# Experts written out, weight stream reordered, outputs summed in PSUM: the mixture-of-experts stage of a two-block transformer kernel

## The chip, the cores and the metric

The kernel runs on one core of a Trainium2 chip. A core has TensorE (PE in the profile, with PEld for its weight loads), VectorE (DVE), ScalarE (ACT), GpSimd (POOL) and SyncE (SP, which issues DMAs), an on-chip memory SBUF of 128 partitions, and PSUM, eight banks of 128 x 512 fp32 into which TensorE writes. Each engine works through its own instructions in order; semaphores tie the engines together. The metric is the device time of one execution in microseconds (us), lower is better.

## The reference

A first block (modulated token mixer with gated delta rule and gated linear attention, then a mixture of experts) and a second block of two attention layers. Only the expert layer matters here: 256 tokens, 32 experts, each token goes to its 4 best; each expert is three 1024 x 1024 fp32 matrices (gate, linear, down), 12 MB.

```
logits = (h @ w_router + b_router)
top_logit, top_idx = lax.top_k(logits, TOP_K); top_p = jax.nn.softmax(top_logit)
# tokens packed by expert, then for each block of tokens xb of expert e:
gu = xb @ w_gu[e] + b_gu[e]
glu = jnp.minimum(gu[:, :D_EXPERT], SWIGLU_LIMIT)
lin = jnp.clip(gu[:, D_EXPERT:], -SWIGLU_LIMIT, SWIGLU_LIMIT)
act = glu * jax.nn.sigmoid(SWIGLU_ALPHA * glu) * (lin + 1.0)
return (act @ w_down[e] + b_down[e]) * p[:, None]
# summed over the experts of each token
```

## The kernel before

`route` computes the router, the gates and each token's rank within its expert. An expert takes up to 64 tokens (SLOTS); tokens beyond that go to a second pass (`further`), which does no expert work in this trace.

`one_pass` runs the 32 experts as a loop on every engine. The weights come as 12 units of 1 MB (512 rows x 512 columns) per expert, in a ring of 12 buffers. To keep fp32 accuracy with the faster fp32r products, each unit is split: ACT copies it, rounded, into one of six `moe_hi` buffers (line 1699); the rest, raw minus hi, is formed in place (line 1488), by DVE for nine units and by POOL for units 2, 6 and 10; then PE multiplies with both parts, 8 matmuls of 512 columns a unit (lines 1522 and 1523). The stationary operand holds the expert's tokens twice, 64 columns of high parts and 64 of low parts.

Around that, for each expert:
- DVE makes the one-hot matrix `pick` of token against slot (line 1588) and `pickg`, the same times the gate (line 1646).
- PE gathers the tokens with `pick` (line 1514, fp32, 32 matmul records for 16 matmuls), ACT and DVE split the result into `moe_xs` (1691, 1601).
- Units 0 to 7 give gate and linear columns, half by half; ACT copies each bank to `gu_tok` (1703), PE transposes (`turn`, 1534), DVE adds the halves and the bias (1608, 1612), clips (1615, 1616), ACT takes the sigmoid (1707), DVE forms the product and splits it into `acs` (1621 to 1627).
- Units 8 to 11 are the down matrix, with `acs` stationary; ACT copies the result to `y_tok` (1687), PE scatters it to the tokens with `pickgT` (1544) and DVE adds it to `yT` in SBUF (1596). Result and scatter of an expert are done inside the next iteration.

The order on each engine is that of the code in each engine's `body`. PE's products of a unit wait for its rest part; ACT's rounding of a unit waits until the unit six places earlier has been used by PE.

## Time and profile before

| | |
|---|---|
| median of 3 runs | 4019.8 us (4016.48 to 4021.62) |
| profiled execution | 4024.09 us, span 4022.3 us |
| granted TensorE clock, mean | 0.854 of full |
| PE busy | 3078.3 us, 77% |
| DVE busy | 2429.5 us, 60% |
| ACT busy | 1645.2 us, 41% |
| POOL busy | 752.9 us, 19% |

The expert stage lies between about 1320 and 2636 us of the span, a third of the kernel. Busy times are of the whole span, so what bounds this stage has to be read from views of the stage alone. A matmul's end in the trace is modelled and matmuls overlap: the distance from start to start is what each one costs.

### The profile page before, as it was taken

The page shows a single profiled execution, that of the slowest core. Times are in us where ns is not written, and L with a number is a line of the kernel's source. Part 1 is how long each engine was busy: PE and PEld are TensorE (multiplying, and loading weights), DVE is VectorE, ACT ScalarE, POOL GpSimd, SP SyncE. Part 2 cuts the span into 40 slices and gives each one's busy share as a digit, 9 for nine tenths or more (in the row PEclk, how much of TensorE's full clock was granted, in tenths as well). Part 3 has the DMA queues.
Part 4 walks back from the last instruction along what each step waited for, and adds up shares of the span by engine and source line. Part 5 has one row for each costly group of instructions (what it writes and reads, how often), then busy time and mean ns, then how long its engine had stood idle before and what let it go on. Part 6 is the DMA issues. An engine that isn't in the chain of part 4 may idle for free. (4 is left out here: it accounts for less than half of the span.)

```text
span 4022.3 us, 51270 instructions
## 1 busy us (share of the span) xinstructions
PE 3078.3 (77%) x17216; PEld 2524.4 (63%) x17217; DVE 2429.5 (60%) x3532; ACT 1645.2 (41%) x2098; POOL 752.9 (19%) x272
## 2 busy tenths in 40 slices
PE   7689999888676788888888888838336987625788
PEld 2368888566476667666767676728224987622688
DVE  1235545343354798989898989845544554454555
ACT  0024444211132576767777777713111442211343
POOL 0022232000000344444544454500000000000000
PEclk9789999877787899999999999969556998755899
DMA  7241100111141888888888888733001542200443
GB/s 261 76 76 32 32 22 1 34 35 59 46 150 49 329 319 315 303 319 302 323 301 321 303 320 299 250 105 111 1 1 51 159 167 84 79 0 0 141 142 104
DMA packets 323602, 605.74 MB, mean 151 GB/s; under 512 B 21858, under 2 KB 79769, under 8 KB 323353
## 3 DMA queue, kind: packets, MB, share of 16 engines
q1 hardware_dynamic: 318300, 598.43, 43.3%
q10 hardware_dynamic: 5181, 5.76, 0.5%
q8 instruction: 68, 1.11, 0.1%
q14 instruction: 53, 0.43, 0.0%
HBM read 599.75 MB, written 4.39 MB: 150 GB/s over the span
## 5 line engine op out<-in xcount | busy, mean ns | idle before, releaser
L1488 POOL TENSOR_TENSOR moe_raw_r<-moe_raw,moe_hi 128x2048 fp32r<-128x2048 f32 x96 | 609.5, 6349 | 1306.3 <-ACT moe_hi L1699 1306.3
L1699 ACT ACTIVATE moe_hi<-moe_raw 128x2048 fp32r<-128x2048 f32 x384 | 708.9, 1903 | 1.9 <-DMA moe_raw<-in_w_gu 1.5
L1488 DVE TENSOR_TENSOR moe_raw_r<-moe_raw,moe_hi 128x2048 fp32r<-128x2048 f32 x288 | 681.5, 2393 | 29.0 <-DVE acs L1627 19.2
L1522 PE MATMUL banks<-moe_hi,moe_xs 128*128 128x512 f32 x1024 | 410.1, 400 | 34.7 <-DVE moe_raw_r L1488 27.7
L1523 PE MATMUL banks<-moe_raw_r,moe_xs 128*128 128x512 f32 x1024 | 401.2, 392 | 0.0
L1522 PE MATMUL banks<-moe_hi,acs 128*128 128x512 f32 x512 | 248.8, 486 | 169.1 <-DVEq L1630 121.0
L319 PE MATMUL banks<-ff_xs,ff_hi 128*128 128x272 f32 x1024 | 300.9, 294 | 70.3 <-DVE ff_raw_r L335 61.0
L321 PE MATMUL banks<-ff_xs,ff_raw_r 128*128 128x272 f32 x1024 | 298.5, 291 | 0.0
L320 PE MATMUL banks<-ff_xs,ff_hi 128*128 128x272 f32 x1024 | 298.0, 291 | 0.0
L1522 PEld LDWEIGHTS banks<-moe_hi,acs 128*128 128x128 f32 x512 | 119.7, 234 | 222.3 <-issue 134.4
L1522 PEld LDWEIGHTS banks<-moe_hi,moe_xs 128*128 128x128 f32 x1024 | 193.3, 189 | 96.0 <-DVE moe_raw_r L1488 41.7
L319 PEld LDWEIGHTS banks<-ff_xs,ff_hi 128*128 128x128 f32 x1024 | 196.0, 191 | 74.2 <-issue 62.3
L1523 PE MATMUL banks<-moe_raw_r,acs 128*128 128x512 f32 x512 | 235.9, 461 | 0.0
L1523 PEld LDWEIGHTS banks<-moe_raw_r,moe_xs 128*128 128x128 f32 x1024 | 193.4, 189 | 38.3
L320 PEld LDWEIGHTS banks<-ff_xs,ff_hi 128*128 128x128 f32 x1024 | 196.5, 192 | 0.0
L321 PEld LDWEIGHTS banks<-ff_xs,ff_raw_r 128*128 128x128 f32 x1024 | 196.2, 192 | 0.0
L732 PE MATMUL banks<-hT,wq 128*128 128x256 f32 (+1 forms) x512 | 181.3, 497 | 4.6 <-PEq L161 2.1
L321 PE MATMUL banks<-sc_r,ring_att_r 128*128 128x272 f32 x608 | 180.2, 296 | 0.0
L319 PE MATMUL banks<-sc_r,PT_r 128*128 128x272 f32 x304 | 94.7, 311 | 91.7 <-DVE ring_att_r L335 88.5
L1707 ACT ACTIVATE sg<-gu 128x256 f32<-128x256 f32 x64 | 26.7, 418 | 323.5 <-DVE gu L1615 323.5
L1646 DVE TENSOR_SCALAR pickg<-con,rankr,gate 128x128 f32<-128x128 f32 x64 | 156.9, 2490 | 0.0
L335 DVE TENSOR_TENSOR ff_raw_r<-ff_raw,ff_hi 128x1024 fp32r<-128x1024 f32 x128 | 156.0, 1219 | 0.0
(471 smaller groups left out, 6553.2 us busy)
## 6 DMA issues: line engine op xcount, KB each, us to landing
moe_raw<-in_w_gu SPq DMA_DIRECT2D x256, 1024.0 KB, 7.9
moe_raw<-in_w_down SPq DMA_DIRECT2D x128, 1024.0 KB, 5.1
ff_raw<-in_w_ff SPq DMA_DIRECT2D x128, 512.0 KB, 3.8
ring_mod<-in_w_mod SPq DMA_DIRECT2D x12, 2048.0 KB, 8.7
wq<-in_w_in SPq DMA_DIRECT2D x32, 512.0 KB, 4.1
ring_att<-in_w_in SPq DMA_DIRECT2D x32, 512.0 KB, 3.7
ring_att<-in_w_in SPq DMA_DIRECT2D x32, 448.0 KB, 3.7
wh<-in_w_in SPq DMA_DIRECT2D x10, 1024.0 KB, 8.5
```

Source lines behind the costliest of these rows:

```text
L319: pe.matmul(ps[m][:, :n], w_hi, x_hi, start=(k == 0), stop=False)
L320: pe.matmul(ps[m][:, :n], w_hi, x_lo, start=False, stop=False)
L321: ins = pe.matmul(ps[m][:, :n], w_lo, x_hi, start=False, stop=(k == KT - 1))
L335: dve.tensor_tensor(lo[:, k, :cols], raw[:, k, :cols], hi[k % RING_HI][:, :cols].bitcast(F32), ALU.subtract).then_inc(los, 1)
L732: ins = pe.matmul(out, wq[:, h % 2, n, k, :], hT[:, k, lo:TOK], start=(k == 0), stop=(k == KT - 1))
L1488: eng.tensor_tensor(rest[u][:, :, :], raw[u][:, :, :], hi[:, u % HI_SLOTS, :, :].bitcast(F32), ALU.subtract).then_inc(sem, 1)
L1522: pe.matmul(bank, x[:, k, :], hi[:, u % HI_SLOTS, k, :], start=first, stop=False)
L1523: ins = pe.matmul(bank, x[:, k, :], rest[u][:, k, :], start=False, stop=last)
L1646: ins = dve.tensor_scalar(pickg[:, t, :], con[:, K_SLOT:K_SLOT + P], rank, gate[:, t, bass.ds(e, 1)], ALU.is_equal, ALU.mult)
L1699: act.activation(hi[:, u % HI_SLOTS, :, :], raw[u][:, :, :], ACT.Copy).then_inc(his, 1)
L1707: act.activation(sg[:, :, :], g[:, 0, :, :], ACT.Sigmoid, scale=ALPHA).then_inc(sig, 1)
```

## The change

The 32 experts are no longer a loop; their code is written out on each engine. A unit is now 256 rows x 1024 columns (still 1 MB). The stream order is a list: after the first expert's gate and linear columns it goes, for each expert e, gate columns of e+1 (g), down matrix of e (d), linear columns of e+1 (u). The first 12 units are issued in `route`. DVE forms all rest parts; POOL has no work in this stage. A pair of PSUM banks (0,1 or 2,3, in turn) takes all products of an expert; banks 4 to 7 collect the output of all experts, first b_down times gates, then each expert's scatter as accumulating matmuls, so that DVE's additions to `yT` go. The gather works on tokens that `route` has already split (32 fp32r matmuls of 64 columns). The transposes of gate and linear columns become matmuls with `fold` that also add high and low halves. `pickg` goes; instead PE transposes `pick` and multiplies the gates into a column per slot (`slots_of`), which ACT uses as the scale when it copies the result. The outputs end as tokens x columns, so a short stage after the loop transposes them back.

```diff
+def stream_order():
+    out = [("g", 0, q) for q in range(4)] + [("u", 0, q) for q in range(4)]
+    for e in range(NEXP):
+        if e + 1 < NEXP:
+            out += [("g", e + 1, q) for q in range(4)]
+        out += [("d", e, q) for q in range(4)]
+        if e + 1 < NEXP:
+            out += [("u", e + 1, q) for q in range(4)]
...
+        def first_units(sp):
+            for n in range(UNITS):
+                load_unit(sp, n)
...
+        def gather(pe, hot_one, bank):
+            for k in range(KT):
+                for x, c in ((h_hi, 0), (h_lo, SLOTS)):
+                    for t in range(2):
+                        ins = pe.matmul(ps[bank + k // 4][:, k % 4 * P + c:k % 4 * P + c + SLOTS], x[:, t, k * P:(k + 1) * P],
+                                        hot_one[:, t, 0:SLOTS], start=(t == 0), stop=(t == 1))
...
+        def slots_of(pe, hot_one, gates, bank):
+            for t in range(2):
+                pe.transpose(ps[bank][:, t * P:(t + 1) * P], hot_one[:, t, :].bitcast(F32), ident)
+            for t in range(2):
+                ins = pe.matmul(ps[bank][:, LAT:LAT + 1], hot_one[:, t, :].bitcast(F32), gates(t), start=(t == 0), stop=(t == 1))
...
+            @block.tensor
...
+                def scatter(e):
+                    pe.wait_ge(y_out, e + 1)
+                    for t in range(2):
+                        for c in range(2):
+                            ins = pe.matmul(ps[4 + 2 * t + c][:, :], pickT[:, t * P:(t + 1) * P], y[:, c * 512:(c + 1) * 512],
+                                            start=False, stop=(e == NEXP - 1))
...
+                for e in range(NEXP):
+                    nxt = e + 1 < NEXP
+                    if nxt:
+                        pe.wait_ge(x_out, e + 2)
+                        for q in range(2):
+                            unit("g", e + 1, q)
+                    turn(e, 1)
+                    if nxt:
+                        for q in range(2, 4):
+                            unit("g", e + 1, q)
+                    pe.wait_ge(t_free, 2 * e + 2)
+                    for q in range(4):
+                        if q % 2 == 0:
+                            pe.wait_ge(act_ready, 2 * e + q // 2 + 1)
+                        unit("d", e, q)
+                    if nxt:
+                        pe.wait_ge(gu_out, 2 * e + 3)
+                        for q in range(4):
+                            unit("u", e + 1, q)
+                            if q == 1:
+                                scatter(e)
+                            if q == 2:
+                                slots_in(e + 1)
+                        if e + 2 < NEXP:
+                            pe.wait_ge(s_out, e + 2)
+                            fetch(e + 2)
+                        pe.wait_ge(gu_out, 2 * e + 4)
+                        turn(e + 1, 0)
...
+            @block.scalar
...
+                def rounded(n):
+                    act.wait_ge(loaded[n % UNITS], n // UNITS * 16 + 16)
+                    if n >= HI_SLOTS:
+                        act.wait_ge(used, n - HI_SLOTS + 1)
+                    act.activation(hi[n % HI_SLOTS][:, :], raw[n % UNITS][:, :], ACT.Copy).then_inc(his, 1)
...
+                for e in range(NEXP):
...
+                    if nxt:
+                        rounded(g0)
+                        if e:
+                            results(e - 1)
+                        for q in range(1, 4):
+                            rounded(g0 + q)
+                    slots_out(e)
+                    rounded(d0)
+                    out("u", e)
+                    rounded(d0 + 1)
+                    if nxt:
+                        x_of(e + 1)
+                    rounded(d0 + 2)
+                    sigmoid(e, 0)
+                    rounded(d0 + 3)
+                    if nxt:
+                        rounded(u0)
+                        out("g", e + 1)
+                        rounded(u0 + 1)
+                    sigmoid(e, 1)
+                    if nxt:
+                        rounded(u0 + 2)
+                        rounded(u0 + 3)
...
+            @block.vector
...
+                for e in range(NEXP):
...
+                    if nxt:
+                        lo(g0, g0 + 1)
+                    act_first(e, 0)
+                    if nxt:
+                        lo(g0 + 2)
+                    act_second(e, 0)
+                    if nxt:
+                        lo(g0 + 3)
+                    act_first(e, 1)
+                    lo(d0)
+                    act_second(e, 1)
+                    lo(d0 + 1, d0 + 2, d0 + 3)
+                    if nxt:
+                        lo(u0)
+                        if e + 2 < NEXP:
+                            dve.wait_ge(slots, e + 1)
+                            hot_of(e + 2)
+                        lo(u0 + 1, u0 + 2, u0 + 3)
...
+        with stage(nc, "yt_sb yt_mm yt_v") as (block, in_sb, mm, on_dve):
```

PE, before, from the gather of the next expert (L1514) to the second transposes (L1534) and the down units, inside the loop body; the REGISTER_ALU and ISA rows compute what is waited for:

```order
L1511 REGISTER_ALU
L1514 MATMUL banks<-pick,htok 128x128 x16
L1561 REGISTER_ALU
L1563 MATMUL banks<-con,pickg 128x128 x2
L1527 REGISTER_ALU
L1529 ISA
L1534 MATMUL banks<-con,gu_tok 128x128 x8
L1566 REGISTER_ALU
L1484 REGISTER_ALU
L1522 MATMUL banks<-moe_hi,acs 128x512
```

PE, after, from the end of the second linear unit through the scatter (L1572), the third unit, the slots (L1518, L1520) to the start of the fourth; further on, the last rows of the gather (L1509) and the turn (L1564):

```order
L1550 MATMUL banks<-moe_raw_r,moe_xs 128x512 x2
L1572 MATMUL banks<-y_tok,pickT 128x512 x4
L1550 MATMUL banks<-moe_hi,moe_xs 128x512 x2
L1550 MATMUL banks<-moe_raw_r,moe_xs 128x512 x2
L1550 MATMUL banks<-moe_hi,moe_xs 128x512 x2
L1550 MATMUL banks<-moe_raw_r,moe_xs 128x512 x2
L1518 MATMUL banks<-con,pick 128x128 x2
L1520 MATMUL banks<-gate,pick 128x1 x2
...
L1509 MATMUL banks<-pick,htok_lo 128x64 x2
L1564 MATMUL banks<-con,gu_tok 128x64 x8
L1550 MATMUL banks<-moe_hi,moe_xs 128x512 x2
```

The scatter, which stood in the middle of an expert's eight gate and linear units, now stands with the slots, the gather and the first turn in the last three linear units and right behind them.

DVE, before, from the last rest part ahead of the additions to `yT` to the second half of the activation:

```order
L1488 TENSOR_TENSOR moe_raw_r<-moe_raw,moe_hi 128x2048
L1593 REGISTER_ALU
L1595 REGISTER_ALU
L1596 TENSOR_TENSOR yT<-yT,banks 128x512
...
L1608 TENSOR_TENSOR gu<-banks,vec 128x512
L1432 ISA
L1612 TENSOR_TENSOR gu<-gu,banks 128x512
L1432 REGISTER_ALU
L1615 TENSOR_SCALAR gu<-gu 128x256
L1616 TENSOR_SCALAR gu<-gu 128x256
L1487 REGISTER_ALU
L1488 TENSOR_TENSOR moe_raw_r<-moe_raw,moe_hi 128x2048
```

DVE, after, from the rest parts of d1, d2, d3 and u0 (the first `x4`), the one-hot rows of the expert after next, u1, then u2, u3 and the next g0 and g1 (the second `x4`) to the first half of the activation, with g2 inside it (rows L1693 are rest parts; `moe_yT_r` is the sixth rounded buffer, `y_tok_r` is the memory of `acs`):

```order
L1693 TENSOR_TENSOR moe_raw_r<-moe_raw,moe_hi 128x2048 x4
L1525 TENSOR_SCALAR pick<-con,rankr 128x128 x2
L1693 TENSOR_TENSOR moe_raw_r<-moe_raw,moe_yT_r 128x2048
L1693 TENSOR_TENSOR moe_raw_r<-moe_raw,moe_hi 128x2048 x4
L1703 TENSOR_TENSOR gu<-banks,vec 128x512
L1707 TENSOR_SCALAR gu<-gu 128x256
L1708 TENSOR_SCALAR gu<-gu 128x256
L1693 TENSOR_TENSOR moe_raw_r<-moe_raw,moe_hi 128x2048
L1713 SCALAR_TENSOR_TENSOR gu<-gu 128x256
L1715 TENSOR_TENSOR gu<-gu,sg 128x256
L1717 CAST y_tok_r<-gu 128x4x64
L1719 TENSOR_TENSOR y_tok_r<-gu,y_tok_r 128x4x64
```

Between the activation of one expert and that of the next DVE now has nothing but rest parts and one pair of one-hot rows; the additions to `yT`, the `pickg` rows and the second addition of halves are gone, and three rest parts an expert have come from POOL.

## Rows read from the trace of the kernel before

**Rows 1.** Stage table: us; busy PE, PEld, DVE, ACT, POOL; clock; DMA share; GB/s

```profile
1336.10:2589.30 1253.20, 1061.05 (x5017) 855.20 (x5017) 1119.49 (x1055) 900.37 (x715) 590.85 (x94) 0.94 0.88 316
```

**Rows 2.** Timeline (start, length, engine, line, operation), ACT, first and 32nd result copy

```profile
1336.10 1.00 ACT L1687 ACTIVATE y_tok<-banks 128x1024 f32<-128x1024 f32 x1
...
2589.28 1.03 ACT L1687 ACTIVATE y_tok<-banks 128x1024 f32<-128x1024 f32 x1 [0.65 <-PE banks L1523]
```

**Rows 3.** Timeline of DVE over one expert; in brackets idle before and its releaser

```profile
2007.88 0.69 DVE L1601 TENSOR_TENSOR moe_xs<-banks,moe_xs 128x512 fp32r<-128x512 f32 x1 [2.76 <-ACT moe_xs L1691]
...
2012.40 0.69 DVE L1612 TENSOR_TENSOR gu<-gu,banks 128x512 f32<-128x512 f32 x1
...
2013.66 2.29 DVE L1488 TENSOR_TENSOR moe_raw_r<-moe_raw,moe_hi 128x2048 fp32r<-128x2048 f32 x1
2015.86 0.42 DVE L1621 SCALAR_TENSOR_TENSOR gu<-gu 128x256 f32<-128x256 f32 x1
...
2017.10 0.42 DVE L1627 TENSOR_TENSOR acs<-gu,acs 128x256 fp32r<-128x256 f32 x1
...
2018.14 4.49 DVE L1488 TENSOR_TENSOR moe_raw_r<-moe_raw,moe_hi 128x2048 fp32r<-128x2048 f32 x2 [0.62 <-DVE acs L1627]
2022.55 4.91 DVE L1646 TENSOR_SCALAR pickg<-con,rankr,gate 128x128 f32<-128x128 f32 x2
2027.38 0.47 DVE L1588 TENSOR_SCALAR pick<-con,rankr 128x128 f32<-128x128 f32 x2
2027.78 6.68 DVE L1488 TENSOR_TENSOR moe_raw_r<-moe_raw,moe_hi 128x2048 fp32r<-128x2048 f32 x3
```

**Rows 4.** Timeline of PE and POOL over the same expert

```profile
2003.48 3.73 PE L1514 MATMUL banks<-pick,htok 128*128 128x128 f32 x32
...
2007.38 1.09 PE L1534 MATMUL banks<-con,gu_tok 128*128 128x128 f32 x8
...
2017.71 0.49 PE L1522 MATMUL banks<-moe_hi,acs 128*128 128x512 f32 x1 [3.78 <-DVEq L1630]
...
2018.61 0.63 PE L1523 MATMUL banks<-moe_raw_r,acs 128*128 128x512 f32 x1
...
2020.89 6.22 POOL L1488 TENSOR_TENSOR moe_raw_r<-moe_raw,moe_hi 128x2048 fp32r<-128x2048 f32 x1 [11.27 <-ACT moe_hi L1699]
...
2023.07 0.39 PE L1522 MATMUL banks<-moe_hi,moe_xs 128*128 128x512 f32 x1
...
2024.88 0.39 PE L1522 MATMUL banks<-moe_hi,moe_xs 128*128 128x512 f32 x1
```

**Rows 5.** Timeline of ACT over the same expert

```profile
2007.74 0.38 ACT L1726 ACTIVATE pickgT<-banks 128x256 f32<-128x256 f32 x1
...
2013.57 0.42 ACT L1707 ACTIVATE sg<-gu 128x256 f32<-128x256 f32 x1 [5.45 <-DVE gu L1615]
...
2015.30 7.32 ACT L1699 ACTIVATE moe_hi<-moe_raw 128x2048 fp32r<-128x2048 f32 x4
...
2023.27 1.03 ACT L1687 ACTIVATE y_tok<-banks 128x1024 f32<-128x1024 f32 x1 [0.65 <-PE banks L1523]
```

**Rows 6.** Timelines of PE: fp32 matmuls of 64 columns, then a scatter

```profile
824.60 0.43 PE L1345 MATMUL banks<-le,lS 128*128 128x64 f32 x2
824.97 0.43 PE L1347 MATMUL banks<-latt,lv 64*128 64x64 f32 x2
...
2598.07 3.61 PE L1544 MATMUL banks<-pickgT,y_tok 128*128 128x256 f32 x16
```

**Rows 7.** Stage table, as rows 1, while the ring first fills

```profile
1350.00:1400.00 50.00, 44.34 (x219) 36.62 (x218) 43.79 (x44) 36.75 (x29) 21.37 (x5) 0.93 1.04 387
```

**Rows 8.** Timeline of DVE at the start and the end of the stage

```profile
1318.62 0.91 DVE L1744 MEMSET banks<- 128x1024 f32 x1 [0.21 <-issue]
1320.43 0.48 DVE L1588 TENSOR_SCALAR pick<-con,rankr 128x128 f32<-128x128 f32 x2 [0.91 <-PEq L161]
...
2635.42 0.69 DVE L1596 TENSOR_TENSOR yT<-yT,banks 128x512 f32<-128x512 f32 x1 [0.18 <-PE banks L1544]
```

## Prediction of the time after

> **What bounds the kernel now.** I read the stage table first, for the stretch of the 32 experts alone. From the first result copy to the 32nd are 31 experts in 1253.2 us [rows 1, 2]: 40.43 us an expert. DVE is busy 1119.49 / 31 = 36.1 us of it, PE 34.2, ACT 29.0, POOL 19.1; the DMAs run at 316 GB/s, while 387 were reached as the ring filled [rows 7]. So the stage is not bound by the weights (12.58 MB at 387 GB/s would be 32.5 us) but by DVE, with 4.3 us of waits per expert on top. The timeline of DVE then shows where the time is [rows 3]: nine rest parts of 2.23 us each (6.68 / 3, 4.49 / 2), 4.91 us for two small `pickg` rows, and waits, 2.76 us for the gathered tokens and 0.62 us at the end of the loop body. A row as small as `pickg` takes 0.24 us when nothing is in its way (`pick`, 0.47 for two); the first `pickg` row begins at 22.55 beside POOL's rest part of 20.89 to 27.11 [rows 3, 4] and ends with it, so it waits for POOL. PE waits 3.78 us for the activation, and right behind that its matmuls last 0.63 instead of 0.39 us: the lower clock, 1.2 GHz [rows 4].
>
> **The change part by part.** Its own time is 4024.1 us for the profiled execution, with a span of 4022.3; the median of the runs, 4019.8, is 4.3 below, and I take that off at the end.
>
> DVE's work per expert: 12 rest parts x 2.235 = 26.8 us (three more than before). An activation half is now one addition and two clips, 1.26 us (from the start of the second addition, 2012.40, to the next rest part, 2013.66), and the four steps behind the sigmoid 1.67 us (2015.86 to 17.52) [rows 3]; two halves are 5.9. `pick` 0.5. Sum 33.2, against 36.1: `pickg` (4.9), the additions to `yT`, one addition of halves and the split of the gathered tokens go, three rest parts come. The change takes 2.9 us of work off DVE. If DVE never waited, the period would be 33.2 us.
>
> PE's work per expert: 12 units x 1.81 (23.07 to 24.88, eight matmuls) [rows 4] = 21.7. Scatter: 4 fp32 matmuls of 512 columns instead of 8 of 256; columns times matmuls stay, so 16 records of 256 in 3.61 [rows 6] become 8 records of 0.44 to 0.45: 3.5 us. Turn: 16 fp32 matmuls, two records each as in all fp32 products, 32 records at the 0.1175 us that a record with a fresh 128-column stationary operand took in the gather (3.73 / 32) [rows 4]: 3.76 for both halves, against 2.2. Slots: 2 transposes at 0.14 (1.09 / 8) and 4 records at 0.1175: 0.75. Gather: 32 matmuls of 64 columns, fp32r. No row has that form. Fewer columns save nothing if loading the 128-column operand is what takes the time: lower bound 32 x 0.06 = 1.9 (the time of 64 fp32 columns out of 0.1175 for 128), upper bound 32 x 0.18 = 5.8 (fp32 records of 64 columns elsewhere, 24.60 to 24.97 for two) [rows 6]. I take 3.6, next to the gather of today, because its loads have the same shape. PE: 33.3 us, no longer far below DVE.
>
> The Trainium skill has a rule on this, in "TensorE: Matmul & The Clock Gate", section "Weight-path perf modes": a stationary operand of 128 columns loads fast when its type is not fp32. If fp32r counted as such, the gather would take its lower bound; the trace has no row that shows it either way.
>
> ACT's work: 12 x 1.84 [rows 5] + 4 copies of 1024 columns at 1.03 + 0.38 + about 0.2 for the slots + 2 x 0.42 = 27.6 us. No bound.
>
> **What is late next.** The three loads are near each other, so the order decides. I follow the queues in the order of the diff from one point: DVE has finished the rest part of u1, the second unit of linear columns.
> 1. PE: u1 1.81, scatter 3.5, u2 1.81, slots 0.75, u3 1.81, gather 3.6, turn 1.88, and 0.25 until its result is seen: 15.4 us until DVE may add the bias. None of it can be passed by: PE's queue is in order.
> 2. Meanwhile DVE has four rest parts that are free (u2, u3, g0, g1), 8.9 us. Then it stands 6.5 us. Before, no wait of DVE for PE's side was over 2.76 us [rows 3]. ACT cannot help: its copy of the slots waits for PE's slots (u2 and the scatter before them), and the roundings behind it, up to the linear-column copy, stand in its queue.
> 3. DVE: addition and clips 1.26, rest part g2 2.24, then the sigmoid. ACT's sigmoid stands behind the rounding of d2, whose buffer is g0's; PE does g0 right after the turn, so 1.81 + 0.2 + 1.84 + 0.42 = 4.3 after the turn, against 3.5 on DVE: a wait of 0.6 to 0.8. Then 1.67 and g3 2.24.
> 4. Second half: 1.26 and d0 2.24 on DVE. The second sigmoid stands behind the gate-column copy (which needs g3 multiplied) and one more rounding: 2.0 + 1.03 + 1.84 + 0.42 = 5.3 after g3's rest part, against 3.5: a wait of 2.0. Then 1.67.
> 5. DVE: d1, d2, d3, u0 8.94, `pick` 0.48, u1 2.24, handing over 0.1.
>
> Steps 3 to 5 are 26.9 us (1.26 + 2.24 + 0.6 + 1.67 + 2.24 + 1.26 + 2.24 + 2.0 + 1.67 + 8.94 + 0.48 + 2.24 + 0.1); with step 1, 42.3 us per expert. DVE works 33.2 of these and waits 9.1. The same walk through the order of before, with the POOL durations of its rows, gives 40.25 against the 40.43 measured, so I trust it to about 1 us. PE waits some 4 us for d1's rest part; its clock will fall there, as it did behind 3.78 us, which makes d1 some 1.7 us longer, and that is hidden, since DVE gives only one unit each 2.24 us.
>
> **The sum.** Before, the stage runs from 1320.4 to 2636.1 [rows 8]: 1315.7 us. After: from the first `pick` to u1 of the second expert about 69 (a gather at the low clock 5.0, copy 1.0, first rounding and rest part 4.1, nine more rest parts 20.1, then u3, slots, gather and turn, some 8, and steps 3 to 5 with about one unit of waits, 27, and 4 for small waits), 30 periods of 42.35 are 1270.5, and from there to the last scatter 36 (steps 1 to 4 without the gather of a further expert, three down units, the copy 1.03, scatter 3.5). That is 1375.5, so +60. The weights of the first 12 units are already there, but they hid behind the gather before too. Behind it comes the new stage that turns the sum back: two copies of 1.03, 16 transposes, the last DVE copies of 0.69 each, about 5, and 1.8 for one more stage border (1318.62 to 1320.43 with the zeroing in it [rows 8]): +7. In `route`, b_down times gates is the same number of fp32 columns; what the eight copies to `yT` and the zeroing free (some 3 us) goes for splitting the tokens: 0, bounds -4 to +4. Total +67: 4091 as profiled, 4087 us as a median. That is slower, by 1.7%.
>
> **Rivals.**
> - *The order hides the waits; DVE works without a gap.* Then 33.2, bounded by the DMAs at 32.5, so about 34 a period: 30 x -8.35 = -250: about 3837 us. For it: DVE's work really shrinks, and POOL no longer stops it. Against: for this PE would have to be ahead of DVE when the turn is due, and step 1 puts 15.4 us of PE work behind a rest part with only 8.9 us of DVE work beside it. Chance 8%; another 6% for a part of it (38 to 40 a period, 3950 to 4015).
> - *Gather at its lower bound.* ACT then ends step 1 (slots, rounding d0, linear copy, rounding d1, tokens' copy), so only 0.65 a period goes: 41.7, 4087 - 20 = 4067 us. 20%.
> - *Waits and work saved balance.* 40.3 a period: 4020 to 4028 with the new stage. 4%.
> - *More PE time in step 1.* If records of 64 columns cost 0.18, gather and turn take 5.8 and 2.9: 45.6 a period, +97: 4184. Or the lower clock reaches into the scatter: 3.4 us of lower clock cost 1.7, +51: 4138. Its mechanism starts with PE's longest wait, which ends three units before the scatter. 14%.
> - The forecast: 48%.
>
> A difference under about 0.2% (8 us) cannot be told from none here. Faster: 8 + 6 = 14% and 1% of the balance; slower the three other cases, 82%; the same 3%. The range leaves out the gap-free rival, its milder form for the most part, and the worst of the PE case: 4030 to 4160. The forecast's own range, from an error of 1 us a period, is 4057 to 4117.
>
> **What would show it.** In the profile after: result copies 42 us apart; DVE's rest parts 2.23 each with no row stretched; DVE's addition of the bias preceded by 6 us of idle, released by PE's `fold` matmuls; two shorter waits for the sigmoid, near 0.6 and 2.0; 8 scatter records in 3.5; PE idle near 4 us before d1. I am wrong if DVE's wait for the turn is under 3 us, if the gather's 32 records take far from 3.6, or if the DMAs reach 370 GB/s in the stage.

## The result, and the profile after

The changed kernel takes 4105.6 us (median of 4 runs, 4096.6 to 4108.2), the kernel before 4020.2 beside it: ratio 1.021, 95% interval 1.0192 to 1.0228. It is slower by 85 us where 67 were forecast (4087, range 4030 to 4160). The profiled span is 4106.4 us against 4022.3, +84.1; all that follows is taken from it.

The stage table over 30 experts (columns as in rows 1), and ACT's first and 31st result copy, which bound it:

```profile
1381.78:2675.17 1293.39, 1118.97 (x5221) 874.11 (x5220) 967.03 (x839) 813.53 (x600) 0.00 (x0) 0.93 0.81 291
```
```profile
1381.78 1.09 ACT L1646 ACTIVATE y_tok<-banks,gate_slot 128x1024 f32<-128x1024 f32 x1
...
2675.17 1.12 ACT L1646 ACTIVATE y_tok<-banks,gate_slot 128x1024 f32<-128x1024 f32 x1 [2.26 <-PE banks L1550]
```

An expert takes 1293.39 / 30 = 43.11 us, before 40.43 [rows 1, 2]. DVE is busy 32.2 us of it (36.1 before): its work did fall, by 3.9 us where 2.9 were reckoned. The DMAs went from 316 to 291 GB/s. Nothing is busier than before but PE (1118.97 / 30 = 37.3 us against 34.2), and the time rose all the same. DVE's timeline over one expert shows where it is, and answers to [rows 3]:

```profile
2002.82 0.69 DVE L1703 TENSOR_TENSOR gu<-banks,vec 128x512 f32<-128x512 f32 x1 [6.53 <-PE banks L1564]
...
2007.04 0.43 DVE L1713 SCALAR_TENSOR_TENSOR gu<-gu 128x256 f32<-128x256 f32 x1 [0.81 <-ACT sg L1651]
...
2016.30 0.42 DVE L1713 SCALAR_TENSOR_TENSOR gu<-gu 128x256 f32<-128x256 f32 x1 [2.05 <-ACT sg L1651]
...
2017.89 8.89 DVE L1693 TENSOR_TENSOR moe_raw_r<-moe_raw,moe_hi 128x2048 fp32r<-128x2048 f32 x4
...
2027.09 2.29 DVE L1693 TENSOR_TENSOR moe_raw_r<-moe_raw,moe_yT_r 128x2048 fp32r<-128x2048 f32 x1
2029.30 8.89 DVE L1693 TENSOR_TENSOR moe_raw_r<-moe_raw,moe_hi 128x2048 fp32r<-128x2048 f32 x4
2045.37 0.69 DVE L1703 TENSOR_TENSOR gu<-banks,vec 128x512 f32<-128x512 f32 x1 [7.18 <-PE banks L1564]
```

The brackets are what to read: 6.53 and 7.18 us for the turn (L1564, the `fold` matmuls), 0.81 and 2.05 for the sigmoids. No row is stretched: the 4.91 us `pickg` row of before is gone, and four rest parts take 8.89. PE's timeline on the way to the second of these turns answers to [rows 4]:

```profile
2000.80 1.98 PE L1564 MATMUL banks<-con,gu_tok 128*128 128x64 f32 x16
...
2020.23 1.22 PE L1550 MATMUL banks<-moe_hi,y_tok_r 128*128 128x512 f32 x2 [3.72 <-DVE moe_raw_r L1693]
2021.25 1.05 PE L1550 MATMUL banks<-moe_raw_r,y_tok_r 128*128 128x512 f32 x2
...
2031.40 3.60 PE L1572 MATMUL banks<-y_tok,pickT 128*128 128x512 f32 x8
2034.43 1.02 PE L1550 MATMUL banks<-moe_hi,moe_xs 128*128 128x512 f32 x2
...
2036.69 0.38 PE L1518 MATMUL banks<-con,pick 128*128 128x128 f32 x2
...
2039.22 0.30 PE L1509 MATMUL banks<-pick,htok_hi 128*128 128x64 f32 x2
...
2042.71 2.62 PE L1564 MATMUL banks<-con,gu_tok 128*128 128x64 f32 x16
2045.09 1.20 PE L1550 MATMUL banks<-moe_hi,moe_xs 128*128 128x512 f32 x2
```

From the scatter to the turn PE has no bracket, in these rows and in those left out between them: it works without a gap while DVE stands. The gather takes 42.71 − 39.22 = 3.49 us for 32 matmuls. Two turns differ, though: from the first matmul of the turn to that of the next unit takes 1.79 us in one (2000.80 to 2002.59), 2.38 in the other (2042.71 to 2045.09). The stage tables of those two stretches say why; the last three figures are the granted clock, the DMA share and GB/s (the first stretch begins 0.2 us into its turn):

```profile
2001.00:2002.70 1.70, 1.70 (x17) 1.70 (x17) 0.00 (x0) 1.02 (x1) 0.00 (x0) 1.00 0.88 349
2042.71:2045.09 2.38, 2.38 (x19) 2.38 (x18) 0.00 (x0) 1.02 (x1) 0.00 (x0) 0.74 0.81 324
```

In the second the clock fell to 1.2 GHz in the midst of the turn, with PE busy 2.38 of 2.38 us and after 3.5 us of gather, also busy throughout. The distances between result copies show how often this happens. Of the 30 periods 11 are 41.8 us: in these the clock stays at 2.4 GHz from the turn until PE's wait ahead of d1. Another 15 are 43.5 to 43.7 us; in 11 of them the clock falls within the turn, in 4 just behind it, in the first unit of gate columns. The last four are 45.0 us, and in them the whole turn runs at 1.2 GHz, in 3.41 us. The first 34 us behind the result copy, in a period of 41.82 us and in the next, of 43.57:

```profile
2245.08:2279.08 34.00, 28.64 (x150) 22.20 (x148) 24.33 (x23) 23.47 (x19) 0.00 (x0) 1.00 0.91 326
2286.90:2320.90 34.00, 30.29 (x150) 23.52 (x148) 22.74 (x23) 23.10 (x19) 0.00 (x0) 0.95 0.86 314
```

At the two ends, DVE's first instruction of the stage and, behind the last scatter (which ends at 2712.4), the first row of the new stage and the first of what follows it; last, that same row in the kernel before:

```profile
1317.59 0.87 DVE L1525 TENSOR_SCALAR pick<-con,rankr 128x128 fp32r<-128x128 f32 x4 [8.17 <-PEq L163]
```
```profile
2715.77 1.94 ACT L1753 ACTIVATE moe_raw<-banks 128x1024 f32<-128x1024 f32 x2 [7.10 <-PEq L163]
...
2730.65 1.67 DVE L1959 SCALAR_TENSOR_TENSOR xT<-moe_yT,modT,xT 128x256 f32<-128x256 f32 x4 [8.89 <-PEq L163]
```
```profile
2644.75 3.25 DVE L1773 SCALAR_TENSOR_TENSOR xT<-yT,modT,xT 128x256 f32<-128x256 f32 x8 [8.64 <-PEq L161]
```

So the stage is 2712.4 − 1317.6 = 1394.8 us against 1315.7 [rows 8], +79; the end, from there to the row of L1959, 18.3 against 8.6, +9.7; it starts 2.8 earlier, and what follows is 1.8 shorter. That is the 84.

### The profile page after: what moved, and what is told of

It reads as the page before. It is cut to its first block and busy times, and to the rows that moved or that the text cites. A ratio compares the mean times of both kernels' runs of the same rounds, so it can differ in the third digit from the quotient of the medians.

```text
span 4106.4 us, 47892 instructions
## 1 busy us (share of the span) xinstructions
PE 3167.4 (77%) x17560; PEld 2563.7 (62%) x17561; DVE 2298.7 (56%) x3325; ACT 1588.5 (39%) x2005; POOL 143.4 (3%) x175
## 5 line engine op out<-in xcount | busy, mean ns | idle before, releaser
L1627 ACT ACTIVATE moe_hi<-moe_raw 128x2048 fp32r<-128x2048 f32 x320 | 607.4, 1912 | 345.5 <-PE banks L1550 345.5
L1693 DVE TENSOR_TENSOR moe_raw_r<-moe_raw,moe_hi 128x2048 fp32r<-128x2048 f32 x320 | 715.3, 2285 | 9.6 <-ACT moe_hi L1627 9.6
L1550 PE MATMUL banks<-moe_raw_r,moe_xs 128*128 128x512 f32 x1024 | 332.7, 407 | 0.0
L1550 PE MATMUL banks<-moe_hi,y_tok_r 128*128 128x512 f32 x508 | 194.0, 468 | 161.2 <-DVE moe_raw_r L1693 161.2
L1550 PE MATMUL banks<-moe_hi,moe_xs 128*128 128x512 f32 x772 | 277.6, 442 | 7.2 <-DVE moe_raw_r L1693 5.3
L1550 PEld LDWEIGHTS banks<-moe_hi,y_tok_r 128*128 128x128 f32 x508 | 107.5, 224 | 212.1 <-DVE moe_raw_r L1693 129.9
L1550 PE MATMUL banks<-moe_raw_r,y_tok_r 128*128 128x512 f32 x512 | 185.8, 449 | 0.0
L1550 PEld LDWEIGHTS banks<-moe_hi,moe_xs 128*128 128x128 f32 x772 | 149.3, 204 | 48.5 <-issue 20.3
L1703 DVE TENSOR_TENSOR gu<-banks,vec 128x512 f32<-128x512 f32 x64 | 44.0, 688 | 226.8 <-PE banks L1564 226.7
L1693 DVE TENSOR_TENSOR moe_raw_r<-moe_raw,moe_yT_r 128x2048 fp32r<-128x2048 f32 x64 | 146.3, 2285 | 0.0
L1564 PE MATMUL banks<-con,gu_tok 128*128 128x64 f32 x1024 | 138.2, 294 | 1.3 <-ACT gu_tok L1635 1.3
```

Of the source, the lines that this page charges most:

```text
L1550: ins = pe.matmul(ps[pair(e) + c][:, :], x[:, k, :], w[:, k * D + c * 512:k * D + c * 512 + 512], start=first, stop=last)
L1564: ins = pe.matmul(ps[pair(e) + h][:, (4 * s + m) * SLOTS:(4 * s + m + 1) * SLOTS], gs[:, s, (4 * h + m) * P:(4 * h + m + 1) * P], fold, st ...
L1627: act.activation(hi[n % HI_SLOTS][:, :], raw[n % UNITS][:, :], ACT.Copy).then_inc(his, 1)
L1693: dve.tensor_tensor(rest[n % UNITS][:, :], raw[n % UNITS][:, :], hi[n % HI_SLOTS][:, :].bitcast(F32), ALU.subtract).then_inc(los, 1)
L1703: dve.tensor_tensor(g[:, :, :, :], ps[pair(e) + h][:, :].rearrange("p (s m n) -> p s m n", s=2, m=4), bgu[:, e, :, 4 * h:4 * h + 4].unsque ...
```

## The experiments

Theory T is the prediction's: the period is a cycle. DVE's rest part of u1 releases PE's leg (u1, scatter, u2, slots, u3, gather, turn), DVE has too little to do beside it and stands, and then works through the rest of the expert. Rivals: D, DVE's own work is the limit, and the three rest parts taken from POOL cost it; B, the weights' transfers or the instruction stream are. All ratios are to the kernel before, run beside each; the times are medians. A period is the mean distance between result copies.

**1. No scatter.** The scatter matmuls of experts 0 to 30 are left out.

```diff
-                    for t in range(2):
+                    for t in range(2 if e == NEXP - 1 else 0):
```

> The changed kernel with the scatter products of experts 0 to 30 left out, so the output lacks their part. Theory T (the period is a cycle through PE's queue: DVE stands 6.5 us because u1, scatter, u2, slots, u3, gather and turn are queued ahead of what it waits for): 3.5 us leave that leg, the wait for the turn falls from 6.5-7.2 to about 3.5, ACT's leg (its copy of the slots, one rounding, the linear-column copy) then ends not far behind, so the period falls by about 3.1, from 43.1 to about 40.0, and the time by about 95 us, to 4010. Rival D (DVE's own work, raised by the three rest parts that POOL had, sets the period): no DVE instruction goes, so 43.1 and 4105 stay. Rival B (the weight transfers set it): 4105 as well, with more idle time of DVE moved to other places.

Measured: 4030.8 us (ratio 1.0034, 1.0023 to 1.0045), period 40.73, so −2.4 of the −3.1 expected. Below are waits of DVE for two turns, and the turn ahead of the first of them:

```profile
2005.56 0.69 DVE L1704 TENSOR_TENSOR gu<-banks,vec 128x512 f32<-128x512 f32 x1 [6.12 <-PE banks L1564]
...
2045.56 0.69 DVE L1704 TENSOR_TENSOR gu<-banks,vec 128x512 f32<-128x512 f32 x1 [3.58 <-PE banks L1564]
```
```profile
2001.87 3.65 PE L1564 MATMUL banks<-con,gu_tok 128*128 128x64 f32 x16
```

At the full clock the wait is the 3.5 expected; in the other expert the turn takes 3.65 us instead of 1.8, at 1.2 GHz. The clock is also why 2.4 came and not 3.1: experts in which it falls only ahead of d1 take 38.8 us here and 41.8 in the changed kernel, 3.0 less. D and B are out as the whole cause: no DVE work and no byte went, and 75 us did.

**2. DVE's order alone.** All four gate-column rest parts ahead of the first addition; those of d0 and d1 each move up one place with them.

```diff
-                        lo(g0, g0 + 1)
+                        lo(g0, g0 + 1, g0 + 2, g0 + 3)
                     act_first(e, 0)
-                        lo(g0 + 2)
+                    lo(d0)
...
```

> The changed kernel, only with DVE taking all four rest parts of the next expert's gate columns ahead of the first addition of the bias (before: two). DVE's work and the bytes are the same. Theory T: 4.5 us of DVE work move beside PE's leg, the wait for the turn falls to about 2, but the wait for the sigmoid grows, since one rest part less stands in front of it; a walk through the queues gives a period lower by 3.3 us, 39.8, and a time of about 4005 us. Rival D: no change, 4105. Rival B: no change, 4105. A third possibility is that PE's wait behind the gate columns merely moves: then within 20 us of 4105.

Measured: 4040.3 us (1.0058, 1.0042 to 1.0075), period 40.96: −2.15 of the −3.3. DVE's three waits:

```profile
2009.44 0.69 DVE L1703 TENSOR_TENSOR gu<-banks,vec 128x512 f32<-128x512 f32 x1 [2.13 <-PE banks L1564]
...
2013.66 0.42 DVE L1713 SCALAR_TENSOR_TENSOR gu<-gu 128x256 f32<-128x256 f32 x1 [0.81 <-ACT sg L1651]
...
2021.88 0.43 DVE L1713 SCALAR_TENSOR_TENSOR gu<-gu 128x256 f32<-128x256 f32 x1 [3.03 <-ACT sg L1651]
```

The turn's wait fell from 6.5 to 2.13, as expected (about 2), and the second sigmoid's grew by 1.0. The same work and the same bytes took 65 us less than in the changed kernel, though not the 100 expected: the order is what costs.

**3 and 4. More bytes.** First a further load of 0.197 MB behind every weight load, then behind every second one.

```diff
                     load_unit(sp, n)
+                    if n > UNITS:
+                        sp.wait_ge(spare_in, 16 * (n - UNITS))
+                    sp.dma_start(spare[:, :], w_gu[order[n][1], 0:P, 0:3 * P]).then_inc(spare_in, 16)
```

> The changed kernel with, behind each of the weight loads past the first twelve, another load of 128 x 384 fp32 (0.197 MB) into an array that nobody reads: 18.75% more bytes in the stage of the experts. Theory T: the stage needs 293 GB/s and then 348, still under the 387 that the kernel before reached in a short stretch, so the time stays within 10 us of 4105 (contention could add up to 0.5 us a period, 15 us). Rival B (the weights' transfers, or the stream of instructions beside them, hold the period at 43.1): the period grows with the bytes, by up to 18% or 7.8 us, 240 us in all.

Measured: 4236.5 us (1.0557, 1.0538 to 1.0575), +131: neither T's 10 nor B's 240. The waits of 1500 to 2500 us, of SyncE's queue and of ACT, show that the experiment made a new bottleneck:

```profile
SPq L1544 <- DMA spare<-in_w_gu: 788.5, 252, 5.2
```
```profile
ACT moe_hi L1633 <- DMA moe_raw<-in_w_down: 78.6, 43, 3.6
```

Each weight load stood in the queue behind a wait (L1544) for the further load before it, so the transfers ran one after the other; ACT then waited for weights, which it never does in the changed kernel. It says nothing about bytes. The second form (`if n % 2: continue`, the wait two units back) mends that.

> The changed kernel with a further load of 0.197 MB behind every second weight load (9.4% more bytes), which waits only for the one two units before it and so no longer ties the weight loads into a chain, as the kernel with one behind every load did (there SyncE waited 788 us of 1000 for the further loads themselves). Theory T: 293 GB/s become 320, below the 387 reached: within 12 us of 4105. Rival B: the period grows with the bytes, by 9.4% of 43.1 or 4.0 us, 4230.

Measured: 4103.5 us (1.0221, 1.0199 to 1.0242), period 43.01. Stage table of 1400 to 2500:

```profile
1400.00:2500.00 1100.00, 948.83 (x4420) 739.39 (x4419) 829.17 (x720) 696.69 (x512) 0.00 (x0) 0.93 0.89 321
```

321 GB/s instead of 292 in the same stretch of the changed kernel, at no cost: the transfers are no bound. B falls.

**5. No POOL, in the kernel before.** All twelve rest parts on DVE.

```diff
-POOL_UNITS = (2, 6, 10)
+POOL_UNITS = ()
```

> The kernel before, with one part of the change alone: all twelve rest parts on DVE, none on POOL. It tells what the added DVE work costs by itself. DVE gets 3 x 2.235 = 6.7 us more and loses the stretched small row (4.9 to about 0.5) and some of its waits for POOL; a walk through the queues of before gives 40.2 against 40.25 a period. Theory T: no cost of this part, within 20 us of 4020 (I expect 4020 to 4035). Rival D: the three rest parts cost what they last, up to 6.7 a period, 4020 + 215 = 4235, and then they explain the slowdown of the whole change.

Measured: 4054.7 us (1.009, 1.0073 to 1.0106), period 41.57, +1.14. That is outside T's 4020 to 4035 (and the 20 us it was given), so T's walk had this part too cheap; it is far from D's 4235 too. The stage table of 1400 to 2500, and DVE's `pickg` rows:

```profile
1400.00:2500.00 1100.00, 893.74 (x4286) 727.47 (x4285) 987.01 (x978) 765.77 (x609) 0.00 (x0) 0.92 0.84 303
```
```profile
2001.80 0.60 DVE L1646 TENSOR_SCALAR pickg<-con,rankr,gate 128x128 f32<-128x128 f32 x2
```

The `pickg` row falls from 4.91 to 0.60 once POOL is idle, which confirms that POOL had held it up. The Trainium skill, "SBUF — State Buffer", section "Who interferes with whom", calls the port pair that DVE and GpSimd share an exclusive lock, held for a whole instruction; these rows agree with it. Three rest parts cost 6.7 and this gives back 4.3; with smaller gains elsewhere DVE is busy 37.3 us (987.01 x 41.57 / 1100) instead of 36.1, and its waits stay at 4.3. In the kernel before, DVE's net gain in work, 1.2 us, went straight into the period. So this part alone costs 37 us there; in the changed kernel, whose DVE is busy 32.2, it can't be added up that way, as the next two show. The changed kernel with POOL forming its three rest parts again was not run, so what they cost there is argued from runs 6 and 7 and not measured.

**6 and 7. The same DVE work in two places.** Two sums of 1024 columns per expert, beside PE's leg (6) and among the down rest parts (7).

```diff
                         lo(g0, g0 + 1)
+                    for r in range(2):
+                        dve.tensor_reduce(junk[:, 2 * e + r:2 * e + r + 1], con[:, 0:1024], AX.X, ALU.add)
                     act_first(e, 0)
...
-                    lo(d0 + 1, d0 + 2, d0 + 3)
+                    lo(d0 + 1, d0 + 2)
+                    for r in range(2):
+                        dve.tensor_reduce(junk[:, 2 * e + r:2 * e + r + 1], con[:, 0:1024], AX.X, ALU.add)
+                    lo(d0 + 3)
```

> The changed kernel with two further DVE instructions per expert (sums over 1024 columns into a column that nobody reads; about 1.1 us each by a rest part's 2.235 for 2048), put where DVE then waits for the turn: behind the rest part of g1, ahead of the first addition of the bias. DVE's work grows by 2.2 us. Theory T: DVE stands 6.5 us there, so the period and the time stay: within 10 us of 4105. Rival D (DVE's work sets the period): +2.2 x 31, 4173.

> The same two further DVE instructions, but among the down rest parts, between d2 and d3. Theory T: this stretch is in the cycle (u1's rest part comes later by the same amount, and with it all of PE's leg), so the period grows by the whole 2.2 us: 4105 + 31 x 2.2 = 4173. Rival D: 4173 as well; the two kernels together tell T from D, since only T has them apart. Rival B: 4105 for both.

Measured: 4097.9 us (1.0196, 1.0179 to 1.0213) and 4206.3 us (1.046, 1.0437 to 1.0482). The row is the same in both; the waits for the turn (us in 1500 to 2500, times, longest) are not. First the kernel with the work beside the leg, then the one with it in the cycle:

```profile
2039.44 2.34 DVE L1732 TENSOR_REDUCE junk<-con 128x1 f32<-128x1024 f32 x2
...
DVE gu L1704 <- PE banks L1565: 109.9, 23, 6.4
```
```profile
2026.75 2.34 DVE L1742 TENSOR_REDUCE junk<-con 128x1 f32<-128x1024 f32 x2
...
DVE gu L1704 <- PE banks L1565: 160.9, 21, 8.5
```

In the changed kernel that wait sums to 160.8 over 23 times. Beside the leg, 160.8 − 109.9 = 51 us of it, 2.2 each time, are filled with work, and the period is 43.01: free. In the cycle nothing is filled and the period is 46.41, +3.3. This is the sharpest of the runs: the same instructions cost 0 or over 100 us by their place alone. The 3.3 is 1.0 more than the added work. That 1.0 is the clock's: four successive experts of run 7 had it at 2.4 GHz from the turn to the wait ahead of d1, and they took 44.14 to 44.17 us, 2.35 more than the 41.8 of such experts in the changed kernel, which is the 2.34 added. The first of them, its result copy, its first 34 us, and the next copy:

```profile
2500.11 1.12 ACT L1647 ACTIVATE y_tok<-banks,gate_slot 128x1024 f32<-128x1024 f32 x1 [1.52 <-PE banks L1551]
...
2544.25 1.12 ACT L1647 ACTIVATE y_tok<-banks,gate_slot 128x1024 f32<-128x1024 f32 x1 [1.41 <-PE banks L1551]
```
```profile
2500.11:2534.11 34.00, 29.00 (x150) 22.50 (x150) 24.32 (x25) 23.59 (x18) 0.00 (x0) 1.00 0.85 293
```

Only 4 of 30 experts are such here, against 11 of 30 in the changed kernel.

**8. A new order on all three engines.** Same instructions; the lines are the orders in short, with `first` and `second` for the two halves of DVE's activation steps, `results` for the result copy and `x` for the copy of the gathered tokens.

```diff
-DVE  g0 g1 first(0) g2 second(0) g3 first(1) d0 second(1) d1 d2 d3 u0 pick u1 u2 u3
+DVE  g0 g1 g2 g3 d0 pick first(0) second(0) first(1) d1 second(1) d2 d3 u0 u1 u2 u3
-ACT  g0 results g1 g2 g3 slots d0 copy_u d1 x d2 sig(0) d3 u0 copy_g u1 sig(1) u2 u3
+ACT  g0 results g1 g2 g3 slots copy_u d0 x sig(0) d1 sig(1) d2 d3 u0 u1 copy_g u2 u3
-PE   g0 g1 turn(1) g2 g3 d0 ...
+PE   turn(1) g0 g1 g2 g3 d0 ...
```

> The changed kernel with the same instructions in another order on three engines. DVE: all four gate-column rest parts, the first down one and the one-hot rows come ahead of the first addition of the bias, the linear-column ones last. ACT: the copy of the slots and the linear-column copy directly behind the gate roundings, each sigmoid one place sooner, the gate-column copy behind the second linear rounding. PE: the second turn ahead of the next gate columns. Theory T (order in the queues, not work, makes DVE stand 9 us per expert): with 11.2 us of DVE work beside PE's leg and nothing of PE between the turns, the walk through the queues gives 33.7 a period; the two kernels with part of the leg eased came out 1.4 to 1.7 above that walk, as PE's clock fell more often, so 35 to 35.5 and a time of 3855 us, between 3830 and 3900: faster than both kernels. Rival D (DVE-bound at 43.1): 4105. Rival B (transfers or instruction stream at their limit near 300 GB/s): 12.58 MB need 42 us, so not under 4060.

Measured: 3883.9 us (ratio 0.9672, 0.9656 to 0.9688), period 35.95: 135 us faster than the kernel before and some 220 faster than the changed one. D and B both put this out of reach. Its stage table, and DVE's waits in one expert:

```profile
1400.00:2500.00 1100.00, 1080.49 (x5213) 882.13 (x5211) 963.15 (x837) 804.13 (x598) 0.00 (x0) 0.93 0.89 335
```
```profile
2033.22 0.69 DVE L1697 TENSOR_TENSOR gu<-banks,vec 128x512 f32<-128x512 f32 x1 [1.64 <-PE banks L1564]
...
2034.73 0.43 DVE L1707 SCALAR_TENSOR_TENSOR gu<-gu 128x256 f32<-128x256 f32 x1 [0.28 <-ACT sg L1648]
```

PE is busy 98% now: the stage has become PE-bound, at 35.3 us of PE per expert.

**9 and 10. Why a unit takes longer.** PE's units took 1.865 us and not 1.81. First the bank order of before, in the changed kernel; then the kernel before with its loop written out.

```diff
-                        for w, first, last in ((hi, ...), (rest, ...)):
-                            for c in range(2):
+                        for c in range(2):
+                            for w, first, last in ((hi, ...), (rest, ...)):
```
```diff
-                with eng.Fori(0, NEXP) as e:
+                for e in range(NEXP):
                     body(e, e, e)
```

> The changed kernel with the eight matmuls of a unit in another order: both products of one PSUM bank (rounded part, rest part) follow each other, as before the change, where the changed kernel goes from bank to bank at every matmul. It is to tell why a unit took 1.865 us (0.2328 a matmul) instead of 1.81 (0.2266). Theory K (changing the bank at every matmul costs 6 ns each): a unit takes 1.81 again; eleven or so units lie in the cycle as PE's leg and its gate columns only in part (three units), so the period falls by 0.2 and the time by 5 to 10 us, to about 4097. Theory L (writing the experts out, or the mere form of the wait, costs it): a unit stays at 1.865 and the time at 4104.

> The kernel before, with one part of the change alone: its 32 experts written out one after the other instead of a hardware loop. Theory T: the loop's border costs 0.6 us of DVE's waits per expert (0.62 ahead of the first rest part) and the addresses' arithmetic little else, so the period falls by 0 to 0.6 us and the time lies between 4000 and 4020. Rival F (the longer instruction stream, 1.80 MB against 1.11 on its queue, slows engines or the weight transfers): slower than 4020, up to 4060.

Measured: 4107.1 us (1.0221, 1.0207 to 1.0235), and 4013.4 us (0.999, 0.9981 to 0.9999, some 4 us less). PE's matmuls of 512 columns at the full clock, first with the old bank order, then twice in the written-out kernel before: behind a wait of PE, and further on in a row of units:

```profile
2003.87 0.40 PE L1550 MATMUL banks<-moe_raw_r,moe_xs 128*128 128x512 f32 x1
...
2004.57 0.40 PE L1550 MATMUL banks<-moe_hi,moe_xs 128*128 128x512 f32 x1
```
```profile
2004.98 0.40 PE L1522 MATMUL banks<-moe_hi,acs 128*128 128x512 f32 x1
...
2005.91 0.39 PE L1522 MATMUL banks<-moe_hi,acs 128*128 128x512 f32 x1
```
```profile
2021.15 0.39 PE L1522 MATMUL banks<-moe_hi,moe_xs 128*128 128x512 f32 x1
...
2022.96 0.39 PE L1522 MATMUL banks<-moe_hi,moe_xs 128*128 128x512 f32 x1
```

Three matmuls in 0.70 us with the old bank order: 0.233 each, as in the changed kernel. In the written-out kernel before, four take 0.93 behind the wait, 0.233 each as well, but eight take 1.81 further on: 0.2266, the figure of the loop. The loop itself has both: 0.233 in the unit behind a wait of 1.51 us at 2011.82, 0.2266 in the units of [rows 4]. The mean over all such distances at the full clock between 1400 and 2500 us is 0.2286 in the loop, 0.2283 written out, 0.2328 in the changed kernel and 0.2329 in run 9. So the written-out code does not bring it. What does is open: the changed kernel's unit has four matmuls on one stationary operand where the old one has two, and it changes the bank within the unit even in run 9 (every second matmul, where the old unit stays in one bank); neither was tried alone.

The period of run 10 is 40.27 instead of 40.43. DVE's wait of 0.62 at the loop's border is gone. So are ACT's table loads, two of 1.28 us in each expert of the loop (55 between 1400 and 2500 us) and none written out, there or in the changed kernel; the prediction's count of ACT's work had none either.

**11 and 12. The new order once more.** With the old bank order (edit as in 9), and with the second turn behind the first gate unit, so that gather and turns are not one stretch.

> The kernel in the new order on three engines (3884 us, period 35.95), with the bank order of its units as before the change too. PE is busy 98% of that stage, so here a unit's time is on the path twelve times. Theory K: 12 x 0.055 = 0.65 a period less, 3884 - 20 = 3864. Theory L: 3884.

> The kernel in the new order (3884 us), with the second turn behind the first unit of gate columns, so that the gather and the two turns are no longer one stretch of matmuls of 64 columns (7.3 us at the full clock) but 5.4 and 1.8 with a unit of 512 columns between. The walk gives the same period (33.73 against 33.69). In the kernel in the new order PE's clock falls to 1.2 GHz in every second expert during the gather and the turns, with no wait in front of it, and stays there for some ten microseconds: 36.36 us of alternating periods (34.5, 37.6). Theory M (such a long stretch of small matmuls brings the clock down): the falls get rarer or shorter, mean period under 35.5, time under 3870. Theory N (the clock falls whatever their grouping): period 35.9 or more, 3880 to 3895.

Measured: 3886.9 us (0.9675, 0.9662 to 0.9688) and 3890.8 us (0.968, 0.9667 to 0.9693), periods 35.95 and 36.10. (The mean of the alternating periods, 36.36 in the second expectation, should read 35.95.) The bank order makes no difference here either. The time and the period of run 12 are those of theory N, but the falls are not the same: the clock falls in every expert, for 3.4 or 6.8 us, where in run 8 it falls in 16 of 30, mostly for 10.2. Summed up, an expert has 5.5 us at 1.2 GHz against 5.0. In the kernel of run 8 two neighbouring experts show what it costs; first the rows of their turns, then the stage tables, gather and turns of each:

```profile
2029.53 7.07 PE L1564 MATMUL banks<-con,gu_tok 128*128 128x64 f32 x32
...
2067.77 3.76 PE L1564 MATMUL banks<-con,gu_tok 128*128 128x64 f32 x32
```
```profile
2025.84:2029.53 3.69, 3.69 (x33) 3.69 (x32) 2.95 (x3) 2.83 (x2) 0.00 (x0) 0.94 1.02 409
2029.53:2036.36 6.83, 6.83 (x34) 6.83 (x34) 4.77 (x10) 3.11 (x3) 0.00 (x0) 0.50 0.92 367
2064.50:2067.77 3.27, 3.27 (x31) 3.27 (x31) 0.43 (x1) 2.80 (x2) 0.00 (x0) 1.00 1.02 410
2067.77:2071.34 3.57, 3.57 (x34) 3.57 (x34) 3.35 (x6) 1.38 (x3) 0.00 (x0) 1.00 1.03 406
```

The same 32 `fold` matmuls take 6.83 us at 1.2 GHz and 3.57 at 2.4, with PE busy throughout in both. What decides between the two experts isn't shown.

## Why the prediction was right, and what it mis-sized

The direction and the mechanism hold, step by step.

- *DVE's work*, 33.2 forecast (some of it handing over): busy 32.2. `pickg` was POOL's doing; run 5 shows it alone. DVE's waits are what grew: 9.1 us an expert forecast, 10.9 measured (43.11 − 32.2).
- *Step 1, PE's leg.* The wait for the turn was to be 6.5; it is 6.5 in one expert, 7.2 in the next. Runs 1, 2, 6 and 7 each touch one side of it and answer in size: less PE in the leg, more DVE beside it, more DVE behind it.
- *Steps 3 and 4*: waits of 0.6 to 0.8 and 2.0 forecast; 0.81 and 2.05 where the clock held. Over all 30 experts the two come to 3.5 a period and the turn's wait to 7.1.
- *PE's terms*: scatter 3.5 forecast, 34.43 − 31.40 = 3.03 to the start of the next unit, whose first pair then takes 0.4 longer; turn 1.88, 1.79 at the full clock; gather 3.6, 3.49; slots 0.75, 37.27 − 36.69 = 0.58. The gather as 64-column fp32r matmuls takes what the 128-column fp32 records of before took (3.73 with the last one's modelled end [rows 4]), 0.11 us each, and not its lower bound of 0.06. The Trainium skill, "TensorE: Matmul & The Clock Gate", section "Weight-path perf modes", says that a stationary operand of 128 columns loads fast when its type is not fp32; the 0.11 us give no sign that fp32r counts as such, and no run here has a fast load to compare it with. PE as a whole was put at 33.3 and is busy 37.3: at a granted clock of 0.93 it loses some 3.0 of 43.1 us by estimate (0.07 x 43.1), which the sum had not.
- *The rivals.* The gap-free one named the right prize and the right reason why it would not come: PE isn't ahead of DVE when the turn is due. Run 8 makes it so, and lands at 3884 against its 3837.

**The term that was off** is the period: 42.35 forecast, 43.11 measured. Over 30 periods that is 23 us; the stage as a whole came out 19 above the forecast (+79 against +60), since its head and end were some 4 shorter. At the full clock an expert takes 41.8, 0.55 under the forecast, although a matmul of 512 columns takes 0.233 us and not 0.2266. The clock then adds 1.3 on the mean. So the two errors offset each other in part, and the 0.76 that is left is smaller than the term that was missed. I let the clock fall only behind PE's wait ahead of d1, where it does (3.72 us, then pairs of 1.05) and is hidden. It also falls in or just behind the turn, in 19 of 30 experts, with no wait before it, and there PE is what all wait for: 1.7 to 1.9 us in 15 of them, 3.3 in 4. The rival with the lower clock had the leg right, but put the fall down to PE's wait, into the scatter, and priced it at 1.7 us in each expert.

Smaller: the new end stage was put at 7 and cost 9.7. The stage border, taken as 1.8 us, is 3.4 here (last scatter 2712.4, first copy 2715.77).

So, of the 84 us, some 79 are the stage of the 32 experts (30 periods longer by 2.68 us are 80). The change took work off the busiest engine, put more of PE's in a row between two of its hand-overs, and left DVE with two rest parts too few beside it.

## What to carry to other kernels

Sum the work between two hand-overs in each in-order queue, not over the period: DVE, the busiest engine before the change, had slack enough in one place to take 2.3 us for nothing, while the same instructions some 16 us earlier in its queue cost 3.3. If a rewrite lowers the bound engine's work and the time rises, look for its longest wait, name the queue that it waits on, and move work across before giving up the rewrite: here the reordered kernel is 3.3% faster than the original. An experiment that adds load must not add a wait in the same queue; run 3 did and measured itself.

## What the runs showed of the hardware

- The granted clock fell to 1.2 GHz inside stretches where PE was busy all the time, in gathers and turns of 128 x 64 matmuls and just behind them, and stayed there for 3.4 us or 6.8 (changed kernel) or mostly 10.2 (run 8); the next expert with the same instructions ran at 2.4 GHz. It also fell behind waits of 3.8 us (before) and 3.7 (changed kernel).
- With a fresh 128 x 128 stationary operand a matmul record of 64 columns took 0.11 us at 2.4 GHz, in fp32r (gather, 3.49 / 32) and in fp32 (turn, 1.79 / 16), as much as an fp32 record of 128 columns [rows 4].
- 512-column matmuls took 0.233 us each behind a wait of PE and 0.2266 further on in the kernel before, in a hardware loop and written out alike; in the changed kernel they stay at 0.233.
- In the hardware loop ACT loaded a table twice an expert, 1.28 us each; with the same code written out it did not.
- Two small DVE rows that took 4.91 us beside a large POOL instruction took 0.60 with POOL idle.
- The DMAs carried 335 GB/s over 1100 us in run 8, and 410 in stretches of 3 us.
